# Seams of a two-stack transformer kernel: three weight tiles on one operand tile, projections ahead of the gates, the norm's scaling on VectorE

## Chip, cores and metric

One NeuronCore of a Trainium2 chip. The time is device microseconds of one launch; the number that counts is the median of the runs shown.

## The reference

The input is `x` of 512 tokens by 1024 features, FP32. The first stack has two layers, each a mixer (`mix`) and a per-layer gate (`ple`):

```python
h = rms_norm(x, norm_pre[l]);  u = h @ w_in[l]          # three attention kinds, gates
y = gates0*(oa @ w_br_a[l]) + gates1*(ob @ w_br_b[l]) + gates2*(oc @ w_br_c[l])
x = x + rms_norm(y @ w_out[l], norm_post[l])
x = x + sigmoid(x @ w_ple_gate[l]) * (p[l] @ w_ple_proj[l])   # p[l]: 512 x 256
```

The second stack is a retention mixer (`ret`), a feed-forward stage with a convolution over tokens (`ffn0`), a dilated attention mixer whose keys and values come from a norm of their own (`dil`), and a second feed-forward stage (`ffn1`):

```python
x = x + rmsnorm(m, norm_mix_post[layer])
u = rmsnorm(x, norm_ffn_pre[layer]) @ w_up;  gate, val = u[..., :2816], u[..., 2816:]
x = x + rmsnorm((gelu(conv(gate)) * val) @ w_down, norm_ffn_post[layer])
```

## The kernel before

Features lie on partitions. `X` is `x_res`, eight tiles (KT = 8) of 128 features by 512 tokens. FP32 products are made of three passes: every operand is split into a high part (`h_hi`, rounded to float32r) and a low part (`h_lo`, the rest), and `kt()` (L644) issues hi·hi, lo·hi and hi·lo into one PSUM bank. One call of `kt()` is a step: one 128x128 weight block against one operand tile.

**Weights.** All blocks lie in DRAM in the order of use, in chunks of eight steps (SLOT = 8), and go through a ring of three slots (RING = 3). SyncE loads a chunk (`w_raw`), ScalarE casts it (`hi()`, L1086, L1094: `w_hi`), GpSimd subtracts (`lows()`, L504, L509: `w_lo`), and TensorE waits on `lo_done` at a chunk's first step. `hi(at)` casts chunks up to `at // 8 + 3`. It may cast a chunk when TensorE has done the chunk three earlier, and it stands in ScalarE's program at fixed places, so a cast comes no earlier than what ScalarE has before it.

**Banks.** Seven PSUM banks rotate; bank 7 (OUTB) takes the sums over partitions (a matmul with `ONES`). `open()` waits until the bank's last tile was evicted. `whole()` (L654) runs the eight steps of one output tile. `together()` (L659) opens several banks and runs, for each operand tile k as it becomes ready (semaphore `operand`), one step for each.

**A seam** is the passage from `linear()` (L817, L1253, L1814) of one stage to the next stage. `linear` makes eight tiles of the residual branch, M1 or M2 (`m`); ScalarE squares each, VectorE adds the squares in TC, and TensorE sums over partitions (L836, L838). All engines wait for each other in `begin_stage`. Then comes the chain: VectorE's variance (`rstd`, L1472), ScalarE's Sqrt (`std`, L1100), VectorE's reciprocal (L1475), GpSimd's eight `m` = `m` · RSTD (L517), VectorE's X = X + m (L1596), ScalarE's high part (L1147, L1149, L1424), VectorE's low part (L1584, L1586, L1581). There are six: into ple0, ple1, ffn0, dil, ffn1, and the end, where X goes out instead.

**ple** runs gate tiles 0 and 1 together, then needs the split of `p` (`PH`, `PL`, 2 tiles, L1463 and L1465), projections 0 and 1 (two steps each), and then gate and projection in turn. **ffn_up** has 22 pairs of gate and value tiles; it runs tiles 0 and 1 together, then tile 2, then the sum of squares of the norm before (`all_squares`, L673, of a sum that VectorE makes with seven adds, L1485). For each pair x VectorE does the convolution, ScalarE the Gelu (L1308), and VectorE the product and split; before Gelu x ScalarE has its `hi()` of the tiles up to 2x+2. **dil** runs three tiles on `h2` (its columns regrouped by token class), then one and the others on `h`, the operand of the keys and values: ScalarE makes `h_hi` (L1427) and VectorE `h_lo` only after all eight `h2` tiles. `turn_values` (L951) waits until VectorE has evicted the first value tile (L2003), which is the fifth in its order.

## Time and profile before

| what | value |
|---|---|
| median of 3 runs (lowest, highest) | 3306.7 us (3305.99, 3308.75) |
| the profiled execution, its span | 3308.05 us, 3306.2 us |
| TensorE busy | 3058.2 us, 92% of the span |
| VectorE, ScalarE, GpSimd busy | 1909.6, 1054.6, 1200.1 us |
| chain that ended last: TensorE, VectorE | 80%, 13% |
| granted TensorE clock, mean | 0.972 of full |
| DMA queues that carry weights | 25.9% of 16 engines' span |

The span is one profiled execution; its own time stands 1.85 us above it. The busy time of TensorE is modelled from the starts of pipelined matmuls, so the gaps between matmuls tell more than the share. A granted clock of 1.00 is 2.4 GHz, 0.50 is 1.2 GHz.

### The profile page before, as it was taken

The numbers are of one execution on the slowest core, as the hardware profiler recorded it, in microseconds if no ns is written. First come the engines' busy times: TensorE is split into PE (matmuls) and PEld (weight loads), VectorE is DVE, ScalarE is ACT, GpSimd is POOL, SyncE is SP. The second block draws the span as 40 slices with busy tenths as digits, with TensorE's granted clock in tenths as the row PEclk, the third lists the DMA queues.
The fourth block names the chain that finished last, engine by engine and source line by source line (L and its number), as shares of the span: only waits on it lengthen the run. The fifth ranks groups of instructions, "written<-read, shape, count | busy, mean of one in ns | idle before, by whom it ended". The sixth has DMA issues, their size and how long they took to land.

```text
span 3306.2 us, 38334 instructions
## 1 busy us (share of the span) xinstructions
PE 3058.2 (92%) x15088; PEld 2362.2 (71%) x15088; DVE 1909.6 (58%) x2974; ACT 1054.6 (32%) x1826; POOL 1200.1 (36%) x520
## 2 busy tenths in 40 slices
PE   5989999979899999789999989998799999979997
PEld 3766777767667777677776868886577777768885
DVE  4676554555765554555444488823666666488832
ACT  3433333234333432332222232223333333332221
POOL 2322333443222334432232444444333333244443
PEclk9999999989999999999999989999899999999998
DMA  5222222313222223232222323331222222223331
GB/s 164 64 77 64 64 77 83 90 51 99 68 74 67 71 76 90 70 98 68 64 64 64 94 70 98 96 96 51 93 77 77 77 71 77 65 69 97 96 96 64
DMA packets 78506, 262.20 MB, mean 79 GB/s; under 512 B 10910, under 2 KB 13598, under 8 KB 78200
## 3 DMA queue, kind: packets, MB, share of 16 engines
q1 hardware_dynamic: 78136, 257.60, 25.9%
q8 instruction: 120, 1.97, 0.2%
q10 hardware_dynamic: 192, 2.16, 0.2%
q14 instruction: 58, 0.48, 0.0%
HBM read 257.56 MB, written 6.09 MB: 80 GB/s over the span
## 4 chain that ended last, share of the span: by engine, by line
PE 80%; DVE 13%; issue 2%; ACT 2%; DMA 1%; SPq 1%; POOL 0%; ACTq 0%; DVEq 0%; POOLq 0%
PE bank L649 24%; PE bank L651 23%; PE bank L650 23%; PE bank L784 2%; PE bank L737 2%; DVE x_res L1596 1%; PE bank L764 1%; PE bank L915 1%; DVE rstd L1475 1%; PE bank L743 1%; DVE sq L1485 1%; PE bank L963 1%; PE bank L1001 0%; ACT w_hi L1094 0%; PE bank L902 0%
## 5 line engine op out<-in xcount | busy, mean ns | idle before, releaser
L509 POOL TENSOR_TENSOR w_lo<-w_raw,w_hi 128x1024 fp32r<-128x1024 f32 x462 | 1120.2, 2425 | 2046.3 <-ACT w_hi L1094 2045.9
L649 PE MATMUL bank<-h_hi,w_hi 128*128 128x512 f32 x2800 | 1152.9, 412 | 133.3 <-DVE h_lo L1586 53.4
L650 PE MATMUL bank<-h_lo,w_hi 128*128 128x512 f32 x2800 | 1107.3, 395 | 0.0
L651 PE MATMUL bank<-h_hi,w_lo 128*128 128x512 f32 x2800 | 1106.4, 395 | 0.0
L1094 ACT CAST w_hi<-w_raw 128x1024 fp32r<-128x1024 f32 x462 | 483.2, 1047 | 1328.2 <-PE bank L651 1287.7
L649 PEld LDWEIGHTS bank<-h_hi,w_hi 128*128 128x128 f32 x2800 | 534.4, 191 | 306.1 <-issue 156.7
L651 PEld LDWEIGHTS bank<-h_hi,w_lo 128*128 128x128 f32 x2800 | 534.3, 191 | 118.9
L650 PEld LDWEIGHTS bank<-h_lo,w_hi 128*128 128x128 f32 x2800 | 535.6, 191 | 106.1 <-issue 4.5
L1833 DVE TENSOR_SCALAR m<-bank,gains 128x512 f32<-128x512 f32 x48 | 36.0, 751 | 337.6 <-ACT ta L1276 200.3
L1214 ACT ACTIVATE probs<-probs,small_columns 128x128 f32<-128x128 f32 (+2 forms) x192 | 101.8, 530 | 249.8 <-DVE small_columns L1631 245.6
L649 PE MATMUL bank<-f_hi,w_hi 128*128 128x512 f32 x352 | 139.2, 396 | 0.0
L650 PE MATMUL bank<-f_lo,w_hi 128*128 128x512 f32 x352 | 139.2, 396 | 0.0
L651 PE MATMUL bank<-f_hi,w_lo 128*128 128x512 f32 x352 | 139.2, 396 | 0.0
L1997 DVE TENSOR_TENSOR tc<-ta,dil_sin 128x512 f32<-128x512 f32 x48 | 119.5, 2489 | 1.6
L1896 DVE TENSOR_TENSOR ta<-ta,gelu 128x512 f32<-128x512 f32 x44 | 87.9, 1998 | 37.0 <-ACT gelu L1308 37.0
L1626 DVE CUSTOM_DVE_ANT_0 probs<-bank,bias 128x256 f32<-128x256 f32 (+3 forms) x128 | 56.3, 440 | 74.0 <-PE bank L737 69.8
L1883 DVE SCALAR_TENSOR_TENSOR conv_out<-conv_in,gains,conv_out 128x512 f32<-128x512 f32 x44 | 97.6, 2218 | 1.6
L517 POOL TENSOR_TENSOR m<-m,rstd 128x512 f32<-128x512 f32 x48 | 75.9, 1616 | 49.2 <-DVE rstd L1475 49.2
L1475 DVE RECIPROCAL rstd<-var 128x512 f32<-128x512 f32 x16 | 53.7, 3353 | 56.9 <-ACT var L1100 56.9
L1224 ACT COPY pt<-bank 128x256 f32<-128x256 f32 (+3 forms) x160 | 55.4, 386 | 73.1 <-PE bank L764 72.5
L651 PEld LDWEIGHTS bank<-f_hi,w_lo 128*128 128x128 f32 x352 | 66.1, 188 | 16.1
L649 PEld LDWEIGHTS bank<-f_hi,w_hi 128*128 128x128 f32 x352 | 66.1, 188 | 16.0
(278 smaller groups left out, 3840.9 us busy)
## 6 DMA issues: line engine op xcount, KB each, us to landing
w_raw<-in_w SPq DMA_DIRECT2D x462, 512.0 KB, 3.6
bias_copies<-bias_vectors SPq DMA_DIRECT2D x12, 320.0 KB, 9.6
x_res<-in_x_t ACTq DMA_DIRECT2D x1, 2048.0 KB, 8.6
bias<-bias_copies SPq DMA_DIRECT2D x8, 256.0 KB, 5.7
bias<-bias_copies SPq DMA_DIRECT2D x16, 128.0 KB, 2.5
out_x<-x_res SPq DMA_DIRECT2D x8, 256.0 KB, 2.0
ple_raw<-in_p_t SPq DMA_DIRECT2D x2, 512.0 KB, 3.6
ret_decay<-in_decay SPq DMA_DIRECT2D x1, 1024.0 KB, 7.6
```

The costliest lines, as they stand in the source:

```text
L509: pool.tensor_tensor(WL[slot][:], RAW[slot][:], WH[slot][:].bitcast(F32), ALU.subtract).then_inc(sems["lo_done"], 1)
L517: pool.tensor_tensor(m[:, k, :], m[:, k, :], RSTD[:], ALU.mult).then_inc(sems["m_scaled"], 1)
L649: pe.matmul(banks[bank][:], WH[slot][:, w], hi[:, k, :], start=start, stop=False)
L650: pe.matmul(banks[bank][:], WH[slot][:, w], lo[:, k, :], start=False, stop=False)
L651: pe.matmul(banks[bank][:], WL[slot][:, w], hi[:, k, :], start=False, stop=stop).then_inc(sems["kt_done"], 1)
L737: ins = pe.matmul(banks[S0 + m][:, 0:blocks * P], AQ[r, q], keys[r, kk], start=True, stop=(kind != "mla"))
L1094: act.copy(WH[slot][:], RAW[slot][:]).then_inc(sems["hi_done"], t.one("hi_done"))
L1214: act.activation(s, s, ACT.Exp, bias=sm(NM + u), accum_out=sm(DEN + u)).then_inc(sems["exped"], t.one("exped"))
L1475: dve.reciprocal(dst[:], VAR[:]).then_inc(sems[name], t.one(name))
L1883: dve.scalar_tensor_tensor(CO[j][:], GE[j][:, 1:SEQ + 1], conv(x, 1), CO[j][:], ALU.mult, ALU.add).then_inc(sems["dve_step"], t.one("dve_s ...
L1896: dve.tensor_tensor(TA[:], TA[:], GL[j][:], ALU.mult).then_inc(sems["dve_step"], t.one("dve_step"))
L1997: dve.tensor_tensor(TC[:], TA[:], DS[:], ALU.mult).then_inc(sems["dve_step"], t.one("dve_step"))
```

## The change

- GpSimd no longer scales `m`. `postnorm` on VectorE does it: scale tile k+1, low part of tile k, add tile k+1. The semaphores `rstd_ready` and `m_scaled` go.
- ScalarE runs a Sqrt on one column (`ROOT`) after the last Square of every `linear`.
- `ple`: the split of `p` moves into `linear` of `post`. All eight projections run first, ScalarE copies them to SBUF (`PP`) and then frees their banks; the gates follow, three together. The last gate is now the stage's last tile.
- `linear` of `post` and `ffn_up` run three tiles together instead of two; the sum of squares in `ffn_up` comes after tile 4 instead of tile 2.
- `dil`: squares are summed by eight matmuls instead of seven adds and one matmul, right after the first three tiles; the squares are written in token order. Key and value high parts are made between the `h2` tiles; two tiles of them run together; variance and Sqrt come earlier, in the midst of the low parts.
- The order of the weights follows.

```diff
@@ GpSimd @@
-            def scale(m):
-                t.up("rstd_ready")
-                pool.wait_ge(sems["rstd_ready"], t.at("rstd_ready"))
-                for k in range(KT):
-                    pool.tensor_tensor(m[:, k, :], m[:, k, :], RSTD[:], ALU.mult).then_inc(sems["m_scaled"], 1)
...
@@ stages @@
-            e.linear(2, KT, "post", l)
+            e.linear(3, KT, "post", l)
@@ TensorE @@
                 def ple(self, l):
-                    t.up("operand", KT)
-                    pair = [self.rotate() for _ in range(2)]
-                    self.together(pair, HH, HL, KT, KT)
                     t.up("operand", 2)
                     pe.wait_ge(sems["operand"], t.at("operand"))
+                    for _ in range(KT):
+                        bank = self.open_for("p_out")
                         for k in range(2):
                             self.kt(bank, PH, PL, k, k == 0, k == 1)
-                    proj()
-                    proj()
-                    for _ in range(2, KT):
-                        self.whole(self.rotate())
-                        proj()
+                    t.up("operand", KT)
+                    t.up("gate", self.gates - t.k.get("gate", 0))
+                    self.together([self.open_for("gate") for _ in range(3)], HH, HL, KT, KT)
+                    for _ in range(3, KT):
+                        self.whole(self.open_for("gate"))
...
                 def ffn_up(self, l):
                     t.up("operand", KT)
-                    pair = [self.rotate() for _ in range(2)]
-                    self.together(pair, HH, HL, KT, KT)
-                    for x in range(2, 2 * FT):
+                    self.together([self.rotate() for _ in range(3)], HH, HL, KT, KT)
+                    for x in range(3, 2 * FT):
                         self.whole(self.rotate())
-                        if x == 2:
+                        if x == 4:
                             self.all_squares(OUTB, SQ2)
...
                     self.together(opened, H2H, H2L, KT, KT)
+                    for k in range(KT):
+                        t.up("dil_squared")
+                        pe.wait_ge(sems["dil_squared"], t.at("dil_squared"))
+                        ins = pe.matmul(banks[OUTB][:], ONES[:], SQD[:, k, :], start=(k == 0), stop=(k == KT - 1))
+                    ins.then_inc(sems["summed"], t.one("summed"))
                     t.up("operand", KT)
...
+                    self.together([self.open(b) for b in DIL_FIRST_BANKS[3:5]], HH, HL, KT, KT)
@@ ScalarE @@
+                    act.activation(sm(ROOT), ONES[:, 0:1], ACT.Sqrt).then_inc(sems["act_step"], t.one("act_step"))
+                    act.wait_ge(sems["act_step"], t.at("act_step"))
...
                 def ple(self, l):
...
+                    def proj_out(k):
+                        hi(n + 2 * k)
+                        act.wait_ge(sems["kt_done"], n + 2 * (k + 1))
+                        act.copy(PP[:, k, :], banks[(base + k) % ROTATION][:]).then_inc(sems["p_out"], t.one("p_out"))
+                    std()
+                    for k in range(5):
+                        proj_out(k)
                     for k in range(KT):
+                        t.up("x_ready")
+                        act.wait_ge(sems["x_ready"], t.at("x_ready"))
+                        act.copy(HH[:, k, :], X[:, k, :]).then_inc(sems["operand_hi"], t.one("operand_hi"))
+                        if k < 3:
+                            proj_out(5 + k)
+                        elif k == 3:
+                            hi(n + 2 * KT)
...
                     self.operands(HH, f"ffnpre{l}", True, SQ2)
+                    self.past(3, KT)
                     self.past(2, KT)
-                    self.past(1, KT)
                     std()
                     for x in range(FT):
-                        if x:
-                            self.past(2 if x > 1 else 1, KT)
+                        if x > 1:
+                            self.past(1 if x == 2 else 2, KT)
...
-                        act.activation(in_class(SQD[:, k, :]), by_class(X[:, k, :]), ACT.Square).then_inc(sems["squared"], t.one("squared"))
-                    for k in range(KT):
-                        act.activation(in_class(HH[:, k, :]), by_class(X[:, k, :]), ACT.Copy, scale=gain("kv", k)).then_inc(sems["operand_hi"], t.one("operand_hi"))
+                        act.activation(SQD[:, k, :], X[:, k, :], ACT.Square).then_inc(sems["dil_squared"], t.one("dil_squared"))
+                        for j in ((k // 2,) if k % 2 else ()) + (tuple(range(KT // 2, KT)) if k == KT - 1 else ()):
+                            act.activation(in_class(HH[:, j, :]), by_class(X[:, j, :]), ACT.Copy, scale=gain("kv", j)).then_inc(sems["kv_hi"], t.one("kv_hi"))
@@ VectorE, postnorm @@
+                    scaled(0)
+                    added(0)
+                    for k in range(KT):
+                        if k + 1 < KT:
+                            scaled(k + 1)
+                        if target is not None:
+                            dve.wait_ge(sems["x_ready"], t.at("x_ready"))
+                            self.lo_tile(k, *target, classes=classes)
+                        if k + 1 < KT:
+                            added(k + 1)
@@ VectorE, linear @@
+                    if name == "post":
+                        t.up("ple_in", 16)
+                        dve.wait_ge(sems["ple_in"], t.at("ple_in"))
+                        for k in range(2):
+                            split(PH[:, k, :], PL[:, k, :], PX[:, k, :], "operand")
@@ VectorE, dilated @@
                     for k in range(KT):
-                        self.lo_tile(k, HH, HL, "kv", True)
-                    all_squares(SQD)
...
+                        if k == 3:
+                            variance(OUTB, D, in_class, by_class)
...
-                    rstd(OUTB, D)
+                    inverse()
```

## Rows read from the trace of the kernel before

**Rows 1.** PE timeline, seams: start, duration, line, operation [idle before <- releaser]

```profile
673.60 0.77 PE L649 MATMUL bank<-h_hi,w_hi 128*128 128x512 f32 x1 [12.94 <-DVE h_lo L1584]
...
690.19 0.50 PE L649 MATMUL bank<-ple_hi,w_hi 128*128 128x512 f32 x1 [1.58 <-DVE ple_lo L1465]
...
1916.40 0.77 PE L649 MATMUL bank<-h_hi,w_hi 128*128 128x512 f32 x1 [12.95 <-DVE h_lo L1586]
...
1938.07 1.12 PE L673 MATMUL bank<-sq,ones 128*128 128x512 f32 x2 [1.23 <-DVE sq L1485]
...
2301.55 0.76 PE L649 MATMUL bank<-h_hi,w_hi 128*128 128x512 f32 x1 [13.27 <-DVE h_lo L1581]
...
2330.26 0.76 PE L649 MATMUL bank<-h_hi,w_hi 128*128 128x512 f32 x1 [8.71 <-POOL w_lo L509]
...
2364.30 1.12 PE L951 MATMUL bank<-ident,rstd 128*128 128x128 f32 x4 [14.08 <-DVE rstd L2003]
```

**Rows 2.** VectorE timeline, first per-layer seam

```profile
663.55 3.35 DVE L1475 RECIPROCAL rstd<-var 128x512 f32<-128x512 f32 x1 [2.06 <-ACT var L1100]
...
671.60 1.75 DVE L1584 TENSOR_TENSOR h_lo<-x_res,h_hi 128x512 fp32r<-128x512 f32 x1
...
680.62 0.68 DVE L1584 TENSOR_TENSOR h_lo<-x_res,h_hi 128x512 fp32r<-128x512 f32 x1
...
692.00 0.69 DVE L1853 SCALAR_TENSOR_TENSOR ta<-ta,bank 128x512 f32<-128x512 f32 x1 [1.86 <-PE bank L651]
...
692.72 0.69 DVE L1855 SCALAR_TENSOR_TENSOR x_res<-ta,x_res 128x512 f32<-128x512 f32 x1
```

**Rows 3.** ScalarE timeline, same seam

```profile
658.89 0.59 ACT L1276 ACTIVATE tb<-bank 128x512 f32<-128x512 f32 x1
...
661.59 1.28 ACT L1100 ACT_TABLE_LOAD   x1 [2.11 <-DVE var L1472]
...
684.35 0.62 ACT L1147 CAST h_hi<-x_res 128x512 fp32r<-128x512 f32 x1 [0.58 <-DVE x_res L1596]
```

**Rows 4.** The page, costliest groups: busy, mean ns | idle before

```profile
L517 POOL TENSOR_TENSOR m<-m,rstd 128x512 f32<-128x512 f32 x48 | 75.9, 1616 | 49.2 <-DVE rstd L1475 49.2
```

**Rows 5.** Windows: stretch, length, PE PEld DVE ACT POOL busy (records), PEclk, DMA, GB/s

```profile
612.00:614.00 2.00, 2.00 (x7) 1.52 (x6) 1.93 (x3) 0.00 (x0) 0.30 (x1) 0.50 0.37 74
...
678.00:680.00 2.00, 0.44 (x2) 0.01 (x1) 2.00 (x2) 0.62 (x1) 1.55 (x1) 1.00 0.00 0
...
2000.00:2100.00 100.00, 100.00 (x443) 82.80 (x442) 81.91 (x73) 24.40 (x29) 45.13 (x19) 1.00 0.32 96
```

**Rows 6.** PE timeline, start of the output projection of the first layer

```profile
611.27 0.47 PE L649 MATMUL bank<-y_hi,w_hi 128*128 128x512 f32 x1 [2.56 <-DVE tb L1742]
```

**Rows 7.** VectorE timeline, first pair of the first feed-forward stage

```profile
1948.90 2.76 DVE L1465 TENSOR_TENSOR f_lo<-ta,f_hi 128x512 fp32r<-128x512 f32 x1
```

**Rows 8.** ScalarE timeline, same stage, second pair

```profile
1954.58 0.63 ACT L1308 ACTIVATE gelu<-conv_out 128x512 f32<-128x512 f32 x1 [6.03 <-DVE conv_out L1885]
...
1955.11 1.98 ACT L1094 CAST w_hi<-w_raw 128x1024 fp32r<-128x1024 f32 x2
```

**Rows 9.** GpSimd timeline, the weight tiles behind those casts

```profile
1956.22 5.31 POOL L509 TENSOR_TENSOR w_lo<-w_raw,w_hi 128x1024 fp32r<-128x1024 f32 x2 [5.12 <-ACT w_hi L1094]
```

**Rows 10.** ScalarE timeline, seam of the dilated stage

```profile
2302.97 1.25 ACT L1424 ACTIVATE h_hi<-x_res,gains 128x512 fp32r<-128x512 f32 x1 [0.96 <-DVE x_res L1596]
...
2317.81 8.94 ACT L1427 ACTIVATE h_hi<-x_res,gains 128x512 fp32r<-128x512 f32 x8
```

**Rows 11.** VectorE timeline, same seam

```profile
2310.79 1.14 DVE L1581 SCALAR_TENSOR_TENSOR h_lo<-x_res,gains,h_hi 128x512 fp32r<-128x512 f32 x1
...
2350.97 0.69 DVE L1994 TENSOR_TENSOR dil_q<-bank,tb 128x512 f32<-128x512 f32 x1
```

**Rows 12.** PE timeline, retention: four sums over an FP32 tile

```profile
1502.00 3.60 PE L922 MATMUL bank<-ret_y,ones 128*128 128x512 f32 x8
```

**Rows 13.** VectorE timeline, the end of the kernel

```profile
3299.69 4.01 DVE L1596 TENSOR_TENSOR x_res<-x_res,m 128x512 f32<-128x512 f32 x3
```

More of the change, by code:

```diff
@@ L122 @@
 TO_LAST = 3 * KT + sum(k for order in ORDER[:12] for _, k in order)
+GATES_OF_MIX = sum(name in ("z", "g0", "g1") for order in ORDER for name, _ in order)
 DIL_FIRST = (0, 3, 6, 1, 2, 4, 5, 7, 8)
@@ L607, in _ @@
                 mine, stage = "stage_pe", 0
-                n, tiles, rot, steps = 0, 0, 0, 0
+                n, tiles, rot, steps, gates = 0, 0, 0, 0, 0
                 def begin_stage(self):
```

153 lines of the change are left out of this document (74 added, 79 removed).

## The prediction

> **What bounds the kernel now.** I read the page first: TensorE is busy for 92% of the span and makes 80% of the chain that ended last, VectorE 13%. So the time is TensorE's work plus the stretches in which it has none. The timeline of TensorE then gives those stretches; the long ones all lie at the seams. Into ple0 TensorE waits 12.94 us and, before the first projection, 1.58 us; into ffn0 12.95 us and 1.23 us before the sum of squares; into dil 13.27, 8.71 and 14.08 us [rows 1]. ple1 and ffn1 repeat ple0 and ffn0. The work between is the same before and after, so I compare when equal counts of steps are done. A pass takes 100 / 443 = 0.226 us at full clock, a step 0.68 us and a whole tile 5.4 to 5.5 us; at clock 0.50 it takes about twice that [rows 5].
>
> What ends the first wait is a chain. In ple0, with L838 over at 660.66 (673.60 less 12.94, [rows 1]): variance 0.7 us like other tile operations, ScalarE's table load 1.28 us, Sqrt, reciprocal 3.35 us, GpSimd's scaling 1.62 us for each tile, VectorE's add and low part [rows 2 to 4]. The low part takes 1.75 us while GpSimd scales and 0.68 us when it is done: VectorE is slowed by the engine that it waits for.
>
> **The chain, new.** ScalarE's last Square ends at 659.48. The table load now follows at once and ends at 660.77 [rows 3], in the shadow of L838. The one-column Sqrt is not in these rows: above nothing and below the 0.62 us of a full tile; I take 0.3 us. All engines enter the next stage only behind it, so the variance starts some 0.65 us after L838 instead of 0.14 us: of 1.28 us 0.8 us are won. The reciprocal ends 5.4 us after L838. VectorE issues an operation 0.60 us after the last where it doesn't wait, 0.72 us where it waits for its own result [rows 2]. A tile is: add 0.68, high part 0.62 (0.72 with a gain), a gap of 0.1, low part 0.6, so 2.05 to 2.2 us; the scaling of the next tile fits into ScalarE's part. The order is serial: the next add stands behind this low part. The first low part ends 8.4 us, the last some 24 us after L838.
>
> The Trainium skill, "ScalarE: Activation LUTs", section "What ACT_TABLE_LOAD costs", puts a drain of about 1380 ns behind the load of 1283 ns. The trace does not agree: load at 661.59 for 1.28 us, and Sqrt directly behind it [rows 3]. By that rule every stage would be entered 1.4 us later; this is a rival below.
>
> **ple0 and ple1.** The projections need only `p`, whose split now costs 2.3 us of VectorE in the eight us in which it waits for the first output tile: nothing. If that cover were gone they would delay the first evictions by 2.3 us, which seven banks hide. TensorE starts the projections 0.9 us after L838. 16 steps take 11 us, so the gates can begin at 12. ScalarE has Sqrt, five copies, one cast, then the high parts; its first high part comes at 8.5 and VectorE's low part ends near 11, slowed by one GpSimd weight tile. Gates together need 2.05 us for each k, the chain gives one in 2.05 us: no wait, or up to 1.5 us in all. The sixth chunk (five before it are 40 steps) is cast only after the eighth high part and is late by 0.6 us. So 40 steps are done at 0.9 + 27.2 + 0.6 = 28.7 us after L838. Before, 16 were done at 690.19 [rows 1], 29.5 us after L838, and 24 more need 16.3: 45.8. That wins 17.1 us. At the stage's end the last tile is now a gate, so Tanh (0.60 us, like other tiles on ScalarE, [rows 3]) stands in front of the last product: 0.6 us back. **16.5 us each, 33.0 in all**; from 12.5 (clock falls at the entrance, chain late) to 18.
>
> Does the clock fall at the entrance? It was at 0.50 behind a wait of 2.56 us [rows 5, 6] and stayed at 1.00 around 678.44, where a wait of 1.7 us lay between two bursts [rows 5]. The gap is now 0.9 us, after one of 0.8: I take no fall; half a clock for 3 us would cost 1.5.
>
> **ffn0 and ffn1.** TensorE starts 8.6 us after L838 instead of 12.95. The clock is low; in ffn0 it was for six us, in ple0 for three; I take a loss of 2.25 us. Three tiles take 2.05 us per k, as fast as the chain, so 24 steps are done at 8.6 + 16.3 + 2.3 = 27.2. Two more tiles: 38.1, then the sum of squares, whose seven adds are long over. Before, the sum began behind 24 steps and its wait at 1938.07, 34.6 us after L838 (1916.40 less 12.95, [rows 1]); two more tiles make 45.5. Won: 7.4 us.
>
> Then something is late. RSTD comes 5.4 us after the sum. Chunks 7 and 8 of the stage (from 0) were cast behind Gelu 1, 9 and 10 behind Gelu 2. Now 7 comes earlier, but 8 still behind Gelu 1, 9 and 10 behind Gelu 2, and TensorE is two tiles further on. Without GpSimd beside it VectorE's first pair takes 5.5 us (7.6 before, its low part 2.76 us under contention, [rows 7]), so Gelu 1 ends 14.5 us after the sum. Casts of 1.0 us and weight tiles of 2.4 to 2.7 us follow [rows 8, 9]: chunk 8 is ready at 18.0, TensorE wants it at 16.4: 1.6 us. Chunk 9 is ready at 25.5, wanted at 23.5: 2.0 us. Chunk 11 is in time, since a pair takes VectorE some 9 us and TensorE 10.9. So 3.6 us go back; from nothing to 7.4. **3.8 us each, 7.6 in all**; 0 to 14.8.
>
> The post projection with three tiles together has no wait for k before or after; ScalarE squares later, seven banks hide it: nothing, at most 1 us either way.
>
> **dil.** The chain with class order is add 0.68, high part 1.22, gap 0.1, low part 1.06 to 1.14 [rows 10, 11]: 3.09 us a tile, serial now. The reciprocal ends at 2293.7, the first `h2` tile is ready at 2297.7, the last at 2319.3, so three tiles end at 2321.5, as before. What changes comes behind. Before, ScalarE's eight key-value parts (8.94 us, [rows 10]) and the casts behind them made TensorE wait 8.71 us. Now four are done between the tiles, and the squares in token order take 0.6 instead of 1.1 us. TensorE first sums squares: 0.90 us each by four in 3.60 us [rows 12], so 7 us, to 2328.4; it pays them where it stood idle. The key-value tiles and casts are ready by then; two tiles and one more end at 2344.7. VectorE's variance stands in front of low parts 4 to 7 and holds them until 2329.7, ready from 2330.8 on; TensorE wants part 4 at 2333.8. Reciprocal from 2334.1 to 2337.5, two scalings to 2338.9, then four rotated evictions and the value tile. They took 13.3 us, from 2350.97 [rows 11] to the turn; with one more GpSimd tile beside, 14.4: `turn_values` at 2353.3 instead of 2364.30 [rows 1]. A wait of about 9 us stays. **11.0 us**; 5 if the serial chain or the row sums stretch, 14 if the evictions meet no contention.
>
> **The end.** Before, eight scalings at GpSimd's pace, last add over at 3303.70 [rows 13]. Now L838 ends at 3283.76, the reciprocal 5.4 later, eight times 0.72 + 0.60 us: 3299.7. **4.0 us**, 3 to 5. Stores follow the last add as before.
>
> **Sum.** 33.0 + 7.6 + 11.0 + 4.0 = 55.6 us. The profiled execution took 3308.05 us (span 3306.2), so 3252.4; the median of the runs is 1.35 below it: 3251. The likeliest case alone spans 3244 to 3259.
>
> **Rivals.**
> - *The weights are in time.* VectorE, free of GpSimd, reaches Gelu 1 and 2 earlier, or the low clock in ffn is short: 7.2 us more and about 1 in dil, 3243. For it: the two waits are only 1.6 and 2.0 us. 0.13.
> - *The bound moves to the supply behind ScalarE.* Longer waits for chunk 8 and 9 with a fall of the clock (3 us a seam more), gates that wait for the serial chain, a clock fall at ple's entrance (2 us a seam), dil at its low end: 3264. For it: hi() stands behind other work in each seam, and 2.56 us of wait were enough for the low clock [rows 6]. 0.17.
> - *The dummy Sqrt costs a drain as well.* The next stage is entered 1.4 us later, six times: 8.3 us, 3259. The load before showed none. 0.06.
> - *Slower than before.* One mechanism: in ffn_up TensorE never gets ahead of casts that wait for Gelu. It must cost more than 55.6 us over 44 pairs, 1.26 us each, so a pair on VectorE over 12.1 us; that gives 3308 and more. Against it: 82% busy VectorE in a stretch with TensorE at 100% [rows 5], a pair of some 9 us. 0.02.
> - *Nothing moves*, since what the seams win is waited for later in the same stages: 3306. It would need the projections not to run in the gap. 0.02.
>
> The forecast has 0.60. The range 3238 to 3270 takes in the bounds of most terms and leaves out about 1 in 8. A difference under 0.2% (6.6 us) can't be told from no change; faster by more 0.96, within 0.02, slower 0.02.
>
> **What the profile after would show.** Right: projections (`ple_hi`) some 1 us behind L838 at clock 1.00, gates directly behind them; first `h_hi` step in ffn 8.6 us behind L838; two waits of 1 to 3 us for GpSimd's `w_lo` near 55 and 62 us behind L838 in each ffn; in dil no wait for `w_lo`, and 8 to 10 us in front of L951; VectorE's low parts at 0.7 us. Wrong: `w_lo` waits over 3 us, a low clock on the projections, a table load that delays the variance by over 1 us, or waits between the k of three tiles in ple.

## The result

The changed kernel takes **3272.39 us** (median of four runs, 3266.02 to 3274.94) against 3307.34 (3305.99 to 3308.75): a ratio of 0.9893, 95% interval 0.9881 to 0.9905. That is faster, by 35 us where 56 were forecast, and 2.4 us above the top of the range of 3238 to 3270. A second series of four gave 3273.2 us, ratio 0.9896 [0.9882, 0.9911].

The windows view of the kernel after, one row a stage (mix0 with its set-up, ple0, mix1, ple1, ret, ffn0, dil, ffn1, end). A stage ends with the norm's sum L838 or, for a per-layer stage, with the first matmul of the next. Columns: stretch, length, busy time (records) of PE, PEld, DVE, ACT, POOL, PEclk, DMA share, GB/s.

```profile
0.00:660.01 660.01, 598.94 (x2840) 443.38 (x2840) 370.12 (x799) 239.45 (x489) 207.52 (x90) 0.98 0.28 86
660.01:724.33 64.32, 55.59 (x242) 44.77 (x241) 47.64 (x44) 27.39 (x42) 25.33 (x11) 0.96 0.22 66
724.33:1335.90 611.57, 589.56 (x2832) 438.98 (x2832) 356.77 (x764) 230.61 (x479) 199.84 (x83) 0.99 0.26 78
1335.90:1400.27 64.37, 55.70 (x242) 44.86 (x241) 47.65 (x44) 27.38 (x42) 25.32 (x11) 0.96 0.23 70
1400.27:1882.52 482.25, 456.53 (x1862) 350.04 (x1862) 219.57 (x236) 129.54 (x164) 155.36 (x64) 0.97 0.25 75
1882.52:2265.78 383.26, 370.80 (x1590) 301.66 (x1590) 234.88 (x229) 99.42 (x118) 161.47 (x67) 0.98 0.29 88
2265.78:2872.33 606.55, 570.44 (x3909) 444.32 (x3908) 392.11 (x654) 208.23 (x406) 196.52 (x87) 0.98 0.24 74
2872.33:3254.35 382.02, 369.32 (x1591) 300.45 (x1590) 234.91 (x229) 96.43 (x115) 154.52 (x64) 0.98 0.28 84
3254.35:3272.83 18.48, 0.00 (x0) 0.00 (x0) 14.49 (x18) 0.95 (x3) 0.00 (x0) 0.63 0.30 114
```

The same cut through three profiles: before (span 3306.2), after (3272.8) and the same kernel once more (label `again`, 3271.5).

| us | before | after | again | forecast gain | gain, after | gain, again |
|---|---|---|---|---|---|---|
| ple0 + ple1 | 154.74 | 128.69 | 128.78 | 33.0 | 26.1 | 26.0 |
| ffn0 + ffn1 | 768.66 | 765.28 | 761.80 | 7.6 | 3.4 | 6.9 |
| dil | 611.65 | 606.55 | 606.27 | 11.0 | 5.1 | 5.4 |
| end | 22.47 | 18.48 | 18.47 | 4.0 | 4.0 | 4.0 |
| mix0, mix1, ret | 1748.71 | 1753.83 | 1756.19 | 0 | -5.1 | -7.5 |

In mix0, mix1 and ret the change edits the ends alone: the one-column Sqrt in all three, and in the mixtures three tiles together and the split of `p`.

TensorE's timeline after, at the seams, answers to [rows 1]. The number in brackets is the wait before the matmul, and behind the arrow stands what ended it:

```profile
660.49 0.47 PE L648 MATMUL bank<-ple_hi,w_hi 128*128 128x512 f32 x1 [0.48 <-ACTq L1108]
...
671.76 0.39 PE L648 MATMUL bank<-h_hi,w_hi 128*128 128x512 f32 x1
...
681.14 0.50 PE L648 MATMUL bank<-h_hi,w_hi 128*128 128x512 f32 x1 [1.03 <-DVE h_lo L1604]
...
724.33 0.77 PE L648 MATMUL bank<-h_hi,w_hi 128*128 128x512 f32 x1 [6.86 <-DVE h_lo L1606]
...
1891.12 0.77 PE L648 MATMUL bank<-h_hi,w_hi 128*128 128x512 f32 x1 [8.60 <-DVE h_lo L1606]
...
1939.91 0.47 PE L648 MATMUL bank<-h_hi,w_hi 128*128 128x512 f32 x1 [1.19 <-POOL w_lo L513]
...
1947.48 0.47 PE L648 MATMUL bank<-h_hi,w_hi 128*128 128x512 f32 x1 [1.84 <-POOL w_lo L513]
...
2275.23 0.77 PE L648 MATMUL bank<-h_hi,w_hi 128*128 128x512 f32 x1 [9.45 <-DVE h_lo L1601]
...
2306.87 0.47 PE L648 MATMUL bank<-h_hi,w_hi 128*128 128x512 f32 x1 [0.91 <-POOL w_lo L513]
...
2337.62 1.12 PE L946 MATMUL bank<-ident,rstd 128*128 128x128 f32 x4 [13.43 <-DVE rstd L2035]
```

The waits of 12.94, 12.95 and 13.27 us of before are 0.48, 8.60 and 9.45. The projections fill the per-layer seam and the gates follow without a gap. What was not in the forecast stands in two of these rows: 6.86 us at the end of ple0, and 13.43 us before the turned values, which in [rows 1] was 14.08 and should have been 9. Two smaller ones go against what the prediction says of the profile: the wait of 1.03 us between steps of the three gate tiles, and the 0.91 us for `w_lo` in dil (under 0.4 in again). The end of ple0 before:

```profile
738.05 0.73 PE L649 MATMUL bank<-h_hi,w_hi 128*128 128x512 f32 x1 [3.59 <-DVE h_lo L1586]
```

The end of ple0 after, ScalarE, GpSimd and VectorE in turn (answers to the VectorE rows at 692.00 in [rows 2]):

```profile
717.56 1.04 ACT L1089 CAST w_hi<-w_raw 128x1024 fp32r<-128x1024 f32 x1 [3.90 <-PE bank L650]
718.51 0.59 ACT L1306 ACTIVATE tb<-bank 128x512 f32<-128x512 f32 x1
```

```profile
718.68 2.34 POOL L513 TENSOR_TENSOR w_lo<-w_raw,w_hi 128x1024 fp32r<-128x1024 f32 x1 [3.04 <-ACT w_hi L1089]
```

```profile
719.13 2.43 DVE L1882 SCALAR_TENSOR_TENSOR tb<-tb,ple_proj 128x512 f32<-128x512 f32 x1 [2.21 <-ACT tb L1306]
721.60 0.69 DVE L1884 SCALAR_TENSOR_TENSOR x_res<-tb,x_res 128x512 f32<-128x512 f32 x1
```

The last Tanh stands behind a weight cast. The cast also starts a GpSimd tile, that is, one subtraction that makes a chunk's `w_lo`. VectorE's product begins inside that tile. It now reads its projection from SBUF and no longer from a bank; it lasts 2.43 us in place of 0.69 and ends 0.54 us behind that tile's end (721.02). Below, such an operation is called held. That pairing is the thread through the rest.

### The profile page after: what moved, and what is told of

Same layout as the page of the kernel before. It is cut to its first block, busy times and chain, and to the rows that moved or that the text cites. A ratio compares the mean times of both kernels' runs of the same rounds, so it can differ in the third digit from the quotient of the medians.

```text
span 3272.8 us, 38357 instructions
## 1 busy us (share of the span) xinstructions
PE 3066.9 (94%) x15102; PEld 2368.5 (72%) x15102; DVE 1918.1 (59%) x3015; ACT 1059.4 (32%) x1848; POOL 1125.9 (34%) x472
## 4 chain that ended last, share of the span: by engine, by line
PE 81%; DVE 12%; ACT 3%; issue 2%; DMA 1%; SPq 1%; POOL 0%; ACTq 0%; DVEq 0%
PE bank L648 24%; PE bank L650 23%; PE bank L649 23%; PE bank L784 2%; PE bank L737 2%; DVE rstd L1490 1%; PE bank L764 1%; PE bank L910 1%; PE bank L743 1%; DVE x_res L1618 1%; ACT w_hi L1089 1%; PE bank L958 1%; PE bank L996 1%; SPq L454 1%; PE bank L897 0%
## 5 line engine op out<-in xcount | busy, mean ns | idle before, releaser
L513 POOL TENSOR_TENSOR w_lo<-w_raw,w_hi 128x1024 fp32r<-128x1024 f32 x462 | 1122.0, 2430 | 2085.6 <-ACT w_hi L1089 2085.6
L649 PEld LDWEIGHTS bank<-f_lo,w_hi 128*128 128x128 f32 x352 | 66.2, 188 | 16.0
```

Source lines behind the costliest of these rows:

```text
L513: pool.tensor_tensor(WL[slot][:], RAW[slot][:], WH[slot][:].bitcast(F32), ALU.subtract).then_inc(sems["lo_done"], 1)
L649: pe.matmul(banks[bank][:], WH[slot][:, w], lo[:, k, :], start=False, stop=False)
```

## The experiments

Medians are of four runs unless said otherwise, beside the kernel before on the same chip (medians 3306.36 to 3307.61). The time of a stage is read from each profile as above. "Half clock" is the length of the stretches at granted clock 0.50 that begin in the stage. Where nothing else is said, a stage or a wait is compared with `again`, and a median with its 3273.2 us.

**again**: the changed kernel, unchanged.

> The changed kernel once more. My theory: of the 6.3 us by which the retention stage is longer after the change (482.25 us against 475.95 us), nearly all is TensorE's clock: it stayed low for 6.8 us instead of 3.4 us behind the same waits of 5 us, and this falls out differently from run to run. Then the retention stage should be between 474 and 484 us here, with the low-clock stretches again in steps near 3.4 us, and single times should spread over some 8 us. Rival: the change slows retention by something that it issues; then the stage is at 482 us again to within 0.5 us, and so in every kernel that has the same instructions there.

The retention stage (ret) was 481.19 us, inside the 474 to 484 expected but only 1.1 from the first profile, so this run alone decides nothing. What it does show is that ffn0 and ffn1 took 381.41 and 380.39 us, 1.9 and 1.6 less than in the first profile of the same kernel, with the same waits of 1.19 and 1.84 us. The windows just behind the longer wait, which ended at 1947.48 in the first profile and at 1949.70 in again:

```profile
1948.60:1951.60 3.00, 3.00 (x9) 2.32 (x8) 2.89 (x4) 0.00 (x0) 1.52 (x1) 0.50 0.67 183
```

```profile
1949.70:1952.70 3.00, 3.00 (x13) 2.51 (x14) 2.89 (x4) 0.00 (x0) 2.67 (x1) 1.00 0.62 173
```

At clock 0.50 (1.2 GHz) TensorE does 9 matmuls in 3 us, at 1.00 (2.4 GHz) 13. The same wait was followed by the low clock once and not the other time.

**tanh_before_cast**: the last Tanh of a per-layer stage ahead of the cast.
```
-                        hi(done)
+                        hi(done - (k == KT - 1))
```


> Leaves the cast of the chunk behind the stage to the next stage, so that the last gate's Tanh is not behind it and GpSimd's weight tile is not beside the last products. My theory: of the 6.86 us that TensorE waits at the end of each per-layer stage, 0.95 us are that cast and 1.75 us the product that reads two SBUF operands while GpSimd runs. Wait falls to 4.2 us, total 5.3 us shorter than the changed kernel. Rival: the wait is the drain of the engines at the stage's end, and only the cast goes, 1.9 us in all, or the next stage waits for its third chunk instead.

Both stages took 61.60 us in place of 64.38, and the wait was 4.12 in place of 6.86: 5.6 us in the two, as expected. The median fell by only 3.0 (3270.2). In the profile ffn0 and ffn1 are 1.8 and 1.6 us longer, with 17.1 and 13.7 us at half clock, where again has 10.2 each.

**supply_earlier**: chunks of the feed-forward seams cast one Gelu sooner.
```
-                        if x > 1:
-                            self.past(1 if x == 2 else 2, KT)
+                        if x:
+                            self.past(1 if x < 4 else 2, KT)
```


> In ffn_up ScalarE casts chunk 8 behind Gelu 0 and chunk 9 behind Gelu 1, one chunk each. My theory: both waits for w_lo (1.19 and 1.84 us) and the low clock behind the second (3.4 us at half rate, 1.7 us lost) go in each of the two stages: 4.7 us each, 9.4 us in all. Rival: GpSimd's tiles now stand beside VectorE's first pair and slow it, so that the waits only move to the next chunks: under 3 us in all.

The rival held: 3272.12, 1.1 us faster where 9.4 were expected. The waits of 1.19 and 1.84 us are gone, one of 1.85 us stands 10 us later; ffn1 is 379.24 against 380.39, ffn0 381.81 against 381.41.

**dil_without_tiles** (one run). GpSimd subtracts only 8 of 1024 columns of chunks 3 to 5 there; the rest of those low parts is left out.

> Leaves out GpSimd's subtraction for chunks 3 to 5 of the dilated stage except for one column in 128 (their low parts are wrong). My theory: low parts 4 to 7 of the keys and values take 10.4 us instead of 4.4 us because GpSimd's three weight tiles run beside them; without them the turn of the values comes 5 to 7 us sooner and TensorE's wait in front of it falls from 13.4 us to some 8 us. Rival: they are slow by themselves (class order, or the variance just read from PSUM); then the low parts stay at 10 us and the wait at 13 us.

3262.86 us. dil took 601.05 in place of 606.27, the wait 8.73 in place of 13.43: the forecast's "about 9". The tiles beside VectorE are what the forecast of 11 us lacked: 5.2 of the 5.6 us. This run also gave what `again` could not: its retention, where nothing is edited, took 475.58 us (below).

**dil_undone**: order and shares of the second mixture's seam as before, the rest as changed.
```
-        stream += beside(*(parts[x] for x in DIL_FIRST[0:3])) + beside(*(parts[x] for x in DIL_FIRST[3:5])) + [parts[x] for x in DIL_FIRST[5:]] if n == 0 else parts
+        stream += beside(*(parts[x] for x in DIL_FIRST[0:3])) + [parts[x] for x in DIL_FIRST[3:]] if n == 0 else parts
...
```


> The second mixture's first stage is as in the kernel before: shares of the tiles, order of the steps, the three stages beside each other; all else as changed. Theory: the seam's gain was bought twice and half lost, so that undoing it gives back about the 5.1 us that it brought: the stage from 606.4 to 611.5 us, the wait in front of the turned values at 14 us again and the waits of 13 and 8.7 us back, the kernel 5 us slower than the changed one (3278). Rival (the part brings its 11 us, and something else in the stage lost 6): the kernel 11 us slower, 3284.

3279.01 us, 5.8 more; the stage took 612.48, 6.2 more, and the waits of 9.70 (for `w_lo`) and 14.09 us are back. The part is worth some 6 us, not 11. (This kernel's profiled execution, 3285.41 us, is the longest of its four; the stage alone is read from it.)

**raw_sooner**: raw chunks 3 to 5 loaded ahead of the stage's angles and masks.
```
-            load(FIRST["dil"] + RING)
+            load(FIRST["dil"] + 2 * RING)
             after(STAGE["dil"])
```


> The raw weights of chunks 3 to 5 of the second mixture are loaded before the transfers of its angles and masks in the DMA queue, where the changed kernel loads them after; at that seam ScalarE's casts of them waited 1.68 us for the transfer. Theory: the casts come 1.7 us sooner, GpSimd's tiles that stand beside VectorE's low parts 4 to 7 move with them, and the turned values come 1 to 2 us sooner; the kernel is 1 to 2 us faster. Rival (what sets the turned values is VectorE's work, which is as long beside the tiles wherever they stand): no difference over 0.5 us in that stage, 606.3.

3268.88. The stage took 602.49, 3.8 us less, twice the 1 to 2 that were expected, and the wait is 10.75. VectorE's low parts 4 to 7, in the changed kernel and here:

```profile
2306.61 10.44 DVE L2009 SCALAR_TENSOR_TENSOR h_lo<-x_res,gains,h_hi 128x512 fp32r<-128x512 f32 x4
2316.97 3.33 DVE L1490 RECIPROCAL rstd<-var 128x512 f32<-128x512 f32 x1
2320.34 2.58 DVE L2108 TENSOR_TENSOR tb<-tb,rstd 128x512 f32<-128x512 f32 x1
```

```profile
2306.75 6.65 DVE L2009 SCALAR_TENSOR_TENSOR h_lo<-x_res,gains,h_hi 128x512 fp32r<-128x512 f32 x4
2313.31 3.35 DVE L1490 RECIPROCAL rstd<-var 128x512 f32<-128x512 f32 x1
2316.70 0.69 DVE L2108 TENSOR_TENSOR tb<-tb,rstd 128x512 f32<-128x512 f32 x1
```

The same four low parts take 10.44 us in the one and 6.65 in the other. From the variance (2306.00 and 2306.14) to the reciprocal it is 10.97 and 7.17 us, for the same instructions; behind it, the first scaling is held in the one and not in the other.

**dil_scaled_on_gpsimd**: at this seam alone GpSimd scales the norm's tiles.
```
+            for k in range(KT):
+                pool.tensor_tensor(M2[:, k, :], M2[:, k, :], RSTD[:], ALU.mult).then_inc(sems["m_scaled"], 1)
...
```


> GpSimd scales the eight tiles at the second mixture's seam alone, as it does there in the kernel before, and its tiles for the weights of chunks 3 to 5 come after... before them in its order; VectorE scales at all other seams. In the run with all scaling on GpSimd that stage was 602.01 us against 606.27, while each other seam was 3 to 6 us longer. Theory (there VectorE is the bound, with scaling, adding, kv parts and the variance, and GpSimd's scaled tiles come in time): the stage is 602 us again, the turned values 4 us sooner, the wait in front of them 10.7 us in place of 13.4, the kernel 4 us faster than the changed one, 3269. Rival (the 4 us there came from where the clock's stretches fell behind a longer stage before it): the stage stays at 605 to 607 us.

3267.96; the stage 602.03, the wait 10.73: as the theory said. The two remedies leave the same wait, and they were not tried together.

**scaling_on_gpsimd**: all norms scaled by GpSimd, VectorE adds.

> GpSimd scales the eight tiles of the norm as in the kernel before, VectorE only adds; all else as changed. Theory: a scaled tile by GpSimd takes 2.2 us and more and a semaphore's way to VectorE, eight of them 18 to 20 us in a row, against 2.05 us a tile for VectorE's chain now; behind the projections TensorE has to wait for them: each of the four seams with a norm's scaling is 2 to 4 us longer, the kernel 8 to 14 us slower than the changed one. Rival (VectorE is the bound at the seam and is relieved by 0.7 us a tile, 5 us a seam): the seams are up to 3 us shorter and the kernel up to 10 us faster.

3283.46, 10.3 slower, inside the 8 to 14 expected. In the profile, which at 3290.17 us is the longest of the four, ple0 and ple1 lost 6.1 and 4.5 us, ffn0, ffn1 and the end 5.2, 3.3 and 3.1, mostly more than the 2 to 4 a seam of the theory; dil gained 4.3. Beside GpSimd's scaling each VectorE operation with two SBUF operands takes 1.77 us:

```profile
668.33 1.78 DVE L1618 TENSOR_TENSOR h_lo<-x_res,h_hi 128x512 fp32r<-128x512 f32 x1
670.04 1.77 DVE L1631 TENSOR_TENSOR x_res<-x_res,m 128x512 f32<-128x512 f32 x1
```

**no_sqrt_ahead**: the one-column square root left out.

> The one-column square root ahead of the norm's, which is to bring its table, is left out. Theory: the table load of 1.28 us comes after the variance again, in front of rstd at both projection seams; since TensorE is busy with the projections there and waits for the scaled tiles only after them, part of it is hidden: rstd, and with it the first scaled tile, 1.3 us later, and the two seams 1.3 us longer each, the kernel 2.6 us slower than the changed one. Rival (what ScalarE does there is hidden behind the projections' and gates' matmuls): the seams stay at 64.3 and 64.4 us. At the two seams of the feed-forward stages nothing stands over rstd, 1.3 us each under either theory, if the same line serves them.

3281.03, 7.8 slower, where 2.6 were expected at the two projection seams and 1.3 more at each feed-forward seam. ple0 and ple1 are 0.2 us longer (hidden behind the projections: the rival, there). In ffn0, dil and ffn1 the first wait is 0.9 to 1.0 us longer (9.55 in place of 8.60 in ffn0), and the end is 1.0 us longer. Most of the rest of the 8.4 us between the two spans goes with half clock: 17.1 us in ffn0 and in ffn1 against 10.2.

**chain_first**: TensorE waits for the norm's first tile before the projections.
```
+                    pe.wait_ge(sems["x_ready"], l * KT + 1)
```


> TensorE waits before the projections of the per-layer input until the first tile of the norm's sum is there, so that they stand behind the norm's chain and no longer beside it; all else as changed. In the changed kernel they begin 0.48 us behind the last sum, the first tile is there at 666.76, 6.6 us behind it. Theory (the term of 33 us comes from this overlap): the projections and the gates begin 6.3 us later, the clock falls behind the wait (1.7 us more at each seam); each seam is 6 to 8 us longer, 70.5 to 72.5 us, and the kernel 12 to 16 us slower than the changed one. Rival (VectorE's chain or the supply behind ScalarE bounds the gates, and the projections only fill a gap that would be there): the seams are under 3 us longer, the kernel under 6 us slower.

```profile
665.41 0.77 PE L648 MATMUL bank<-ple_hi,w_hi 128*128 128x512 f32 x1 [7.10 <-DVE x_res L1619]
```

The two stages took 73.40 and 73.17 us, 9.0 and 8.8 more, over the 6 to 8 expected; the wait is 7.10 in place of 0.48. Half clock was 17.1 us in each, against 10.2. So without the overlap 17.8 of the 26 us gained in the per-layer stages are gone: it is the large term of the change. The kernel was only 10.8 us slower (3283.97, under the 12 to 16 expected), since its retention took 476.12, 5.1 less than in again.

**before_again** (one run): the kernel before.

> The kernel before once more, for the part of its stages that the change doesn't touch. Theory: the stretches at half clock behind a wait of some 5 us last 3.4 or 6.8 us by chance of when they begin; the retention stage then lies anywhere between 475 and 483 us in the kernel before too, and the stages need not agree with the first profile (475.95). Rival: the retention stage is 476 us within 0.5 in every run of this kernel, and the 5 us that the changed kernel lost there are the change's.

3307.58. ret was 476.10, every other stage within 0.5 us of the first profile. This spoke for the rival, that the change itself makes the retention longer; with dil_without_tiles and chain_first the picture is another. Of 14 profiles with whole tiles four have a retention of 475.6 to 476.1 us (the kernel before twice, dil_without_tiles, chain_first) and ten one of 480.9 to 482.6. In the four the low clock at the stage's start ended within 3.6 us of it, in the ten 5.0 us or later. Some 135 us into the stage the four have a wait of 1.7 us and the ten one of 5.16. Windows behind the stage's first long wait, dil_without_tiles and then again:

```profile
1444.70:1447.90 3.20, 2.88 (x9) 2.50 (x10) 0.95 (x2) 0.59 (x1) 0.00 (x0) 0.50 0.49 163
1448.20:1451.40 3.20, 3.20 (x16) 2.65 (x15) 0.00 (x0) 0.00 (x0) 0.00 (x0) 1.00 0.00 0
```

```profile
1444.20:1447.40 3.20, 1.31 (x5) 1.25 (x6) 1.89 (x3) 0.16 (x1) 0.56 (x1) 0.50 0.47 134
1447.60:1450.80 3.20, 3.20 (x9) 2.47 (x8) 0.40 (x1) 0.23 (x1) 0.00 (x0) 0.50 0.06 20
```

And what stands before the wait of 5.16 us in again, VectorE and then GpSimd:

```profile
1534.59 2.60 DVE L1948 TENSOR_TENSOR ret_k<-ta,ret_cos 128x512 f32<-128x512 f32 x1
1537.22 0.69 DVE L1950 TENSOR_TENSOR tc<-tb,ret_sin 128x512 f32<-128x512 f32 x1
...
1540.12 2.71 DVE L1958 TENSOR_TENSOR ret_k<-ret_k,tc 128x512 f32<-128x512 f32 x1
```

```profile
1534.24 2.39 POOL L513 TENSOR_TENSOR w_lo<-w_raw,w_hi 128x1024 fp32r<-128x1024 f32 x1 [5.32 <-ACT w_hi L1089]
1539.67 2.61 POOL L513 TENSOR_TENSOR w_lo<-w_raw,w_hi 128x1024 fp32r<-128x1024 f32 x1 [3.04 <-ACT w_hi L1089]
```

Each GpSimd tile catches one operation of VectorE, which ends 0.56 and 0.55 us after the tile (1536.63, 1542.28). In dil_without_tiles the second tile begins after this chain's last such operation, and one is caught. Whether a tile catches an operation hangs on when TensorE frees a chunk, and that in part on the clock. The clock also acts by itself. Counted from the stage's start, the second wait ends at 123.5 us in again and at 121.1 in dil_without_tiles, with the same waits up to there: 2.4 us lost at half clock. The third wait is 3.4 us longer. Together that is about the 5.6 us between the two stages.

**seams_without_tiles** (one run): in ple0 and ret, and for the chunks loaded ahead behind each, GpSimd subtracts 8 of 1024 columns; the rest is left out.

> Leaves out, in the first per-layer stage and in the retention stage, GpSimd's subtraction for the low parts of the weights but for one column in sixteen; the second per-layer stage keeps it and stands beside it as a control. Theory (an operation of VectorE with two operands in SBUF that begins beside a tile of GpSimd's lasts until that tile ends, 2.4 to 2.9 us in place of 0.69): no such operation is over 1 us in the first per-layer stage and in the retention; the first seam is 64.4 minus 1.7 at its end minus 1.0 for the wait of 1.03 us, 61.7 us, the second stays at 64.4; the wait of 5.16 us in the retention stage is 1.9 us or less whether the clock's first stretch there is 3.4 or 6.8 us long, and the stage lasts 473 to 477 us. Rival (those operations are slow by themselves, or the retention stage lost its 5 us by the clock alone): the first seam is within 0.5 us of the second; the retention stage stays at 480 us or more when its first slow stretch is 6.8 us.

3232.83 us. ret, ple1, and the last product in ple1, which was 2.43 us long in the changed kernel's ple0:

```profile
1393.62:1840.97 447.35, 444.39 (x1862) 342.17 (x1862) 169.25 (x236) 129.49 (x164) 17.16 (x64) 0.99 0.26 81
...
1331.01:1393.62 62.61, 55.59 (x241) 44.74 (x241) 42.28 (x44) 27.42 (x42) 18.80 (x11) 0.98 0.23 72
...
1390.16 0.69 DVE L1884 SCALAR_TENSOR_TENSOR tb<-tb,ple_proj 128x512 f32<-128x512 f32 x1 [4.01 <-ACT tb L1308]
```

The retention was expected at 473 to 477 and is 447: TensorE has no wait over 0.9 us in it. VectorE is busy for 169 us where it was 220. I had thought of one wait of 5.16 us; the three others of over 5 us (5.16, 5.49 and 5.48 in again) are gone as well. ple0 took 60.56 (61.7 expected); its wait of 1.03 us between two gate steps is gone too, while ple1, which keeps its tiles there, has one of 1.06. ple1 was meant as a control at 64.4 and came to 62.61, because the tile at its end is one for the retention and so among those left out: the product there took 0.69 us and the wait fell from 6.87 to 5.12, the 1.75 us that the held operation costs at the end of a per-layer stage.

**tiles_in_quarters** and **tiles_in_halves**: the same subtraction in four or two instructions.
```
-                    pool.tensor_tensor(WL[slot][:], RAW[slot][:], WH[slot][:].bitcast(F32), ALU.subtract).then_inc(sems["lo_done"], 1)
+                    w = SLOT * P // 4
+                    for x in range(4):
+                        ins = pool.tensor_tensor(WL[slot][:, x * w:(x + 1) * w], RAW[slot][:, x * w:(x + 1) * w],
+                                                 WH[slot][:, x * w:(x + 1) * w].bitcast(F32), ALU.subtract)
+                    ins.then_inc(sems["lo_done"], 1)
```


> Each of GpSimd's 462 tiles of 128x1024 elements (2.43 us) is done as four instructions of 128x256; the same work. Theory (VectorE's operation with two SBUF operands is held until the GpSimd instruction beside which it begins has ended): it is held 0.7 us at most in place of 2.4, though it may be held by several in turn; VectorE's 0.69 us operations beside tiles come to 1.2 us or less, and the retention stage, which was 481 us with the tiles and 447 us without, falls to 450 to 465 us; the kernel is 10 to 30 us faster than the changed one. Rival (both engines share a path word by word and each merely runs slower beside the other): the mean of those operations stays, the stage stays at 476 to 482 us, and the kernel is as fast or, by what four instructions cost more than one on GpSimd, slower.

> Each tile of GpSimd is done as two instructions of 128x512. Theory (held until the instruction ends): held 1.25 us at most in place of 2.4; the retention stage at 460 to 472 us, about half of what quarters give. Rival (a shared path, word by word): no change of over 1 us in any stage but for the clock's stretches.

Quarters took 3241.48 us, 31.7 faster than the changed kernel (10 to 30 expected); ret 465.13 (just outside the 450 to 465). Halves took 3258.71; ret 476.08, less of a gain than expected: 5.1 us, not half of quarters' 16.1. The chain above with quarters, and the busy times of VectorE and GpSimd over the retention:

```profile
1509.50 0.80 DVE L1952 TENSOR_TENSOR ret_k<-ta,ret_cos 128x512 f32<-128x512 f32 x1
1510.34 1.12 DVE L1954 TENSOR_TENSOR tc<-tb,ret_sin 128x512 f32<-128x512 f32 x1
...
1514.09 1.10 DVE L1962 TENSOR_TENSOR ret_k<-ret_k,tc 128x512 f32<-128x512 f32 x1
```

```profile
1384.81:1849.94 465.13, 448.70 (x1862) 343.63 (x1862) 200.44 (x236) 129.70 (x164) 209.42 (x255) 0.99 0.25 78
```

An operation is held for 0.4 us and not for 1.9, at times two in a row. If the engines merely shared a path, cutting the same traffic in four would give nothing. Nor is the gain one of weights that come sooner, which the runs with tiles left out could not rule out: here a tile is 1 us longer. For GpSimd pays: 209 us busy, 156 with whole tiles; a tile of four is 3.4 us long. ffn0 and ffn1 each have waits of 2.3 and 2.2 us for low parts and lose 3.4 each.

**three_mended** (Tanh, supply, raw chunks; whole tiles) and **mended_and_quarters**.

> Tanh before the cast at the end of the per-layer stages, the cast's chunks earlier at the feed-forward seams, and the raw weights of the second mixture sooner, all three, the tiles whole. Theory (the three lie in different stages and add up): 5.6 + 2.4 + 3.8 us less than the changed kernel's 3273.2, so 3261.4, give or take 4 for the clock's stretches. Rival (a gain ahead only moves the clock's stretches and is lost behind it): 3266 or more.

> The three mended parts and the tiles in quarters together. Theory: since quarters already shorten the operation at the end of the per-layer stages and those beside the tiles at the second mixture, the sum is some 4 us short of the two gains added; 8 us below the kernel with quarters alone. Rival (quarters give nothing): as the kernel with the three mended parts.

3263.25 and 3235.31 us: 9.9 of the expected 11.8, and 6.2 below quarters of the expected 8. The gains nearly add up, and ret in the first of them stays at 481.89.

**before_in_quarters** and **mended_in_parts**: the kernel before with quarters; and the mended one with a tile as eight instructions in the mixtures and the retention, four in ple and dil, two in the feed-forward stages.

> The kernel before with GpSimd's tiles for the weights in quarters and nothing else changed. Theory (the contention lies in the mixtures and the retention, which the change does not touch, and the change's gain is its own): 25 to 35 us faster than before, 3272 to 3282, and the change on top of it (tiles_in_quarters, 3241.5) is worth the same 30 to 40 us as it is with whole tiles. Rival (the change only buys off a part of the same contention): before in quarters comes within 15 us of the changed kernel in quarters.

> The three mended parts, with the tiles as eight instructions of 128x128 in the mixtures and the retention, as four in the per-layer stages and the second mixture, as two in the feed-forward stages. Theory (shorter holds where VectorE bounds, whole supply where GpSimd's tile is waited for): the mixtures 2 to 4 us shorter each than with quarters, the retention 2 to 5 us, 3223 to 3231 in all against 3235.3. Rival (what an instruction costs on GpSimd by itself, (3.5 - 2.43) / 3, some 0.36 us, makes a tile of eight 5 us long, and TensorE waits for its low parts): the retention or the mixtures are longer than with quarters, the kernel 3237 or more.

The kernel before falls by 24.5 us to 3281.89, short of 25; the change on top of it is worth 40.4 us, just over the 30 to 40 expected. So the change's gain is its own, and not a way of buying off the same contention. The second kernel is **the best: 3207.16 us (3206.22 to 3207.55), ratio 0.9697 [0.9683, 0.9711]** to before, better than the 3223 to 3231 expected. Its retention:

```profile
1381.05:1831.55 450.50, 444.63 (x1862) 341.38 (x1862) 184.14 (x236) 130.49 (x165) 265.71 (x502) 1.00 0.26 81
```

The gain on mended_and_quarters is 17 us in the retention, and 3 each in dil and the two feed-forward stages. The mixtures, where 2 to 4 us were expected, gave 1.7 and 0.7. In dil the tiles are in four in both kernels, so its 3 us are not explained; half clock there is 17.1 us against 23.9.

## Why the prediction was right and where it failed

**The chain and the projections: right.** The table load follows the last Square, and the Sqrt of one column the load (ScalarE, after; answers to [rows 3]):

```profile
658.85 1.28 ACT L1272 ACT_TABLE_LOAD   x1
660.15 0.20 ACT L1272 ACTIVATE small_columns<-ones 128x1 f32<-128x1 f32 x1
```

So the drain that a rival charged isn't there. The lead was forecast as 0.8 us and is 0.9 to 1.0 where nothing hides it (no_sqrt_ahead). The projections run 0.48 us behind the sum at full clock, the gates directly behind them. Up to its last matmul ple0 won 73.80 - 57.46 = 16.3 us of the forecast 17.1. The wait of 1.03 us at 681.14 stands behind a held scaling (677.59, 2.89 us in place of 0.69), is gone without tiles and accounts for the difference; the forecast had allowed for up to 1.5. chain_first shows that the overlap carries the gain.

**The end of the per-layer stage: the step by which Tanh "stands in front of the last product: 0.6 us back" failed.** It is 3.27 us (6.86 against 3.59): Tanh's 0.6, 0.95 for the cast in front of it, and 1.74 for the held product, two costs that the forecast left out. tanh_before_cast takes back 2.75 of it, the missing tile in ple1 1.75; the two overlap, since the earlier Tanh also puts the product ahead of the tile. Over two stages that is 5.3 of the 6.9 us missed there.

**The feed-forward stages: right mechanism; the size was right in some executions.** In sum 7.6 were forecast, 3.4 came in the first profile and 6.9 in the second. The waits came where they were foretold, 3.03 us for 3.6. In the first profile a low clock behind the 1.84 us wait took 1.9 and 1.6 of it; the forecast had put that into a rival. Of eight profiles with the same code there, four have the two stages at 761.8 us together and four at 763.6 to 765.3.

**dil: the step from low parts 4 to 7 "ready from 2330.8 on" to "Reciprocal from 2334.1" failed.** It took the four low parts as undisturbed, 4.4 us. They began when forecast (40.8 us behind the stage's start, for 41.4) and took 10.4, since the casts of chunks 3 to 5 and so the tiles came beside them. The reciprocal began at 51.2 us for 45.8. The two scalings behind it took 3.2 us for 1.4, one of them held. The rest, "with one more GpSimd tile beside, 14.4", was right: 14.0. Without the three tiles the wait is 8.73 us, for the 9 forecast (dil_without_tiles); with earlier raw weights 3.8 of the 5.6 us come back.

**The end: right**, 4.0 us.

**What the sum had as nothing: "The work between is the same before and after" failed too.** The instructions are the same but for the ends of the mixtures; their time is not: 5.1 to 7.5 us were lost in mix0, mix1 and ret, most of it in ret. The retention has two times 5 to 6 us apart, and where the profiles part, they do so by the clock (2.4 us) and by an operation that a tile catches or not (3.4 us). That the same code lies at 475.58 and 481.19 is shown. That the change makes the longer one more likely is not, and why remains open. The longer wait at the end of ple1, which could shift the low clock, doesn't decide it: chain_first and dil_without_tiles have the wait of 6.87 us and the short retention, tanh_before_cast has 4.12 and the long one (481.86). In mix1 the clock goes with the time: 611.6 us in the first profile with 15.9 us of low clock inside the stage, 614.9 in again with 23.2, 612.1 before with 17.1.

The profile after shows 33.4 us of the 55.6, so 22 are missing. Held operations are about half of them by the runs: 3.5 us at the ends of the per-layer stages, 2.1 in the two waits between gate steps, 5.2 in dil. The casts before the last Tanh are 1.9, the low clock behind the waits in the feed-forward stages 3.5, and the retention's 6.3 are in part one and in part the other. The forecast took the slow low parts beside GpSimd [rows 2, 7] mainly as something that the scaling brought and that would go with it. It charged a weight tile in two places, but not as what any tile does to any VectorE operation with two operands in SBUF that begins in it. Its rival of a supply that bounds, 3264, names the low clock and dil at its low end and is still 8 us short.

The Trainium skill says it, "SBUF — State Buffer", section "SBUF: two separate sides": the pair of ports that both engines use is locked by whichever comes first for its whole instruction, and the other is blocked. The traces agree: the four held operations read here end 0.53 to 0.56 us after the tile. It holds for the whole profile of again. Of VectorE's elementwise operations on 128x512 elements, 237 with two SBUF operands begin inside a tile. Eight of these begin in its last 0.12 us and last 0.7 us; the other 229 last 1.3 to 3.1 us. Operations with a single SBUF operand are held as well (24, at 1.8 to 2.8 us in place of 0.43 to 0.69). An operation that reads or writes a bank is not held: 114 begin inside a tile and none is over 1.1 us. The two kinds side by side in again; the tile lies from 1526.53 to 1528.93:

```profile
1527.24 0.69 DVE L1945 TENSOR_TENSOR tb<-bank,rstd 128x512 f32<-128x512 f32 x1
1527.96 1.50 DVE L1948 TENSOR_TENSOR ret_q<-ta,ret_cos 128x512 f32<-128x512 f32 x1
```

That is why moving the projections from banks to SBUF had a price, 1.74 us a stage, where the forecast saw none.

## What to carry to other kernels

Where VectorE's mean for an operation is well over the least time of its kind, lay GpSimd's instructions beside it: each of GpSimd's can hold one of VectorE's until it ends. Shorter GpSimd instructions took most of that back here (34 us were to be had in the retention, 31 came by cutting in eight). That pays where GpSimd has time to spare and nobody waits for its tile; elsewhere keep them long. When a value moves from a bank to SBUF, count the held operation, and what stands before its producer in that engine's queue.

## What was not expected of the hardware

- One subtraction of 128x1024 took 2.43 us, as two instructions 2.8, as four 3.4, as eight 4.2 (means of one instruction: 2430 ns in the changed kernel, 1417 in halves, 856 in quarters, 521 in mended_in_parts).
- The retention, the same code in many of these kernels, differed by 6 us between profiles with whole tiles, and fell by 34 us with the tiles away; a wait of 1.84 us was followed by the low clock in one profile and not in another of the same kernel.
